# Three weight steps instead of one beside the samples' small mLSTM products, and a wait on two scored key groups ahead of decode's value loads

## The chip, the cores and the metric

The program runs on one core of a Trainium2 chip. The metric is device time in microseconds for one execution. TensorE (PE) multiplies matrices into PSUM banks, ScalarE (ACT) and VectorE (DVE) move and combine values, GpSimd (POOL) does elementwise work and issues some transfers, and SyncE (SP) issues most transfers. Each engine runs its own program in order; they meet at semaphores.

## The reference

One layer of a hybrid decoder on 512 prompt tokens and on 8 sequences of 8 new tokens each ("the samples", 64 rows). The parts that matter here, cut down:

```python
h = rmsnorm(x, g_pre_mix);  z = h @ w_in            # D_MODEL 1024; split into qa ka va qm km vm om, gates
# mLSTM branch, 4 heads of 128; for the samples one chunk of 8 tokens per sequence, with a state C0, n0, m0
A   = einsum('bthd,bshd->btsh', qc, kc) * wD
num = einsum('btsh,bshd->bthd', A, vc) + w_prev[..., None] * einsum('bhde,bthe->bthd', C, qc)
den = sum(A, axis=2) + w_prev * einsum('bhd,bthd->bth', n, qc)
hc  = num / maximum(abs(den), exp(-m_t))[..., None]
# attention of the samples: 2048 cached positions in 16 pages of 128 rows, found by a page table;
# blocks of 256 keys, the 3 best blocks by mean key are attended, plus the new tokens
s = einsum(q, cache_k[pages]) ; p = softmax(chosen blocks and own) ; out = p @ cache_v[pages]
# then both branches are merged by gates, and a squared-ReLU MLP follows
```

## The kernel before

All products with weights are done in three fp32r passes: a weight tile of 128x512 is loaded into one of four slots by SP, ACT rounds it to its high part (line 336), DVE subtracts to get the low part (line 347), and PE multiplies. This is one **weight step**. In the six chunks of `tokens_chunk` (keys, values, output gates of the mLSTM, then queries, keys, values of the attention: `TOKEN_CHUNKS`), a weight step is twelve 128x512 matmuls for the prompt (line 462) and two for the samples (line 470). There are 6 x 8 = 48 such steps. ACT and DVE prepare weights three steps ahead of PE.

The mLSTM itself is done beside these steps. It is written as three generators, one for each of PE, ACT and DVE (`pe_mlstm`, `act_mlstm`, `dve_mlstm`). After each weight step an engine runs its generator up to the next `yield`, so a `yield` is the place of one weight step, and what stands between two of them is one **piece**. The three generators must keep the same number of yields, so that what PE computes in a piece is read by ACT and DVE in theirs. The pieces use PSUM banks 5 to 7 in turn, in the order of a table (`M_USES`); the weight steps use banks 0 to 4. Two uses matter here: `sden` is the samples' denominators (lines 1400 and 1402), `snum` their numerators: four products of the weighted scores `sA` with the values `vm` (line 1407), then eight products with `sqC`, the state's share, four for each half "a" and "b" (line 1415). POOL runs its own list (`pool_mlstm`), released by semaphores.

Evictions of a whole chunk (`act_tokens`, `dve_tokens`) stand at every eighth step, whatever the pieces are. Late in the list ACT issues three output transfers for the samples' states (lines 1573 to 1576); while it issues them it rounds no weights.

After the projections comes the prompt's attention (`pe_prompt`), with matmuls of the gates woven in (line 897), and then decode, the samples' attention over the cache (`pe_decode`). Decode goes over 8 x 4 **groups** of four key pages, one group for each slot s. In slot s PE scores group s-1 (line 1935), transposes the four pages of group s (line 1926, in two halves), and six slots later multiplies with the values (line 1967). Keys lie in a ring `kring` of two groups, values in a ring `vring` of two groups. SP loads the keys of group s+2 when `k_free` says that group s is transposed:

```python
for s in range(DSLOTS):
    if s + 2 < ALL_GROUPS:
        eng.wait_ge(sem("k_free"), s + 1)
        pages(eng, cache_k, kring, "k_in", (s + 2) // GROUPS, (s + 2) % GROUPS)
    for r in fetched_in(A_SLOTS + s):
        sp_step(eng, n, r)
```

ACT copies a group's scores out of PSUM (line 2033) and raises `p_S` by one. POOL loads the values in `pool_values`, eight pages as soon as the prompt's attention is over (both halves of the ring are empty), and then four whenever PE frees a half (`v_free`). Nothing else stands behind these loads on POOL until the merge after decode. Each page is 128 rows of 2 KB, 256 KB in all, and its address is read from the page table at line 1891 before it is issued at line 1893.

Of the kernel before, what the change touches and what calls it, by code (L numbers as in the profile page):

```python
# [94 lines left out]
def moba_mlstm_step(  # L95
# [184 lines left out]
    def sem(name):  # L280
        if name not in names:
            names[name] = stack.enter_context(nc.semaphore(name))
        return names[name]
# [411 lines left out]
    def pe_project(eng, n):  # L695
        first_half_in(eng)
        features_chunk(eng, n, hT, KT, early={0: lambda: first_turn(eng, n, PT), EARLY - 1: lambda: second_half_in(eng)})
        features_chunk(eng, n, hT, KT, 1)
        for b in (5, 6, 7):
            eng.wait_ge(sem(f"free{b}"), n[f"free{b}"].value())  # L700
        side = pe_mlstm(eng)
        for _ in TOKEN_CHUNKS:
            tokens_chunk(eng, n, hT, KT, side=side)
        for _ in side:
            pass
        for b in (5, 6, 7):
            eng.wait_ge(sem(f"m_free{b}"), len(M_USES[b - 5::3]))
# [94 lines left out]
    def act_project(eng, n):  # L802
        for _ in range(KT):
            w_high(eng, n)
        for b in range(8):
            if b % 2 == 0:
                drain(eng, n, b)
                drained(eng.activation(qmT[:, b // 2, 0:HALFT], ps[:, b, 0:HALFT], ACT.Copy), n, b)
            else:
                skip(n, b, b == 7)  # L810
        for _ in range(KT):
            w_high(eng, n)
        eng.wait_ge(sem("small_in"), 64)
        for h in range(2):
            drain(eng, n, h, h == 1)
            c = slice(h * HALFT, (h + 1) * HALFT)
            eng.activation(rf[:, c], ps[32:32 + HM, h, 0:HALFT], ACT.Copy).then_inc(sem("r_in"), 1)
            drained(eng.activation(ri[:, c], ps[0:HM, h, 0:HALFT], ACT.Identity, bias=bif[:, 0:1]), n, h)  # L818
        side = act_mlstm(eng)
        for first in TOKEN_CHUNKS:  # L820
            for k in range(KT):
                w_high(eng, n)
                if k == KT - 1:
                    act_tokens(eng, n, first)
                next(side, None)
        for _ in side:
            pass
    def dve_project(eng, n):
        for _ in range(KT):
            w_low(eng, n)  # L830
        for b in range(8):
            if b % 2 == 1:
                drain(eng, n, b, b == 7)
                drained(eng.tensor_copy(qmT[:, b // 2, HALFT:NT], ps[:, b, 0:HALFT]), n, b)
            else:
                skip(n, b)
        for _ in range(KT):
            w_low(eng, n)
        for h in range(2):
            skip(n, h, h == 1)  # L840
        side = dve_mlstm(eng)
        for first in TOKEN_CHUNKS:
            for k in range(KT):
                w_low(eng, n)
                if k == KT - 1:
                    dve_tokens(eng, n, first)
                next(side, None)
        for _ in side:
            pass
# [363 lines left out]
    def m_bank(use):  # L1213
        return 5 + M_USES.index(use) % 3

    def m_take(eng, use):
        eng.wait_ge(sem(f"m_free{m_bank(use)}"), M_USES.index(use) // 3)
        return m_bank(use)

    def m_full(ins, use):  # L1220
        ins.then_inc(sem(f"m_full{m_bank(use)}"), 1)

    def m_read(eng, use):
        eng.wait_ge(sem(f"m_full{m_bank(use)}"), M_USES.index(use) // 3 + 1)
        return m_bank(use)

    def m_freed(ins, use):
        ins.then_inc(sem(f"m_free{m_bank(use)}"), 1)

    def m_emptied(eng, use):  # L1230
        eng.wait_ge(sem(f"m_free{m_bank(use)}"), M_USES.index(use) // 3 + 1)

    def heads_of(b, n, r=P):
        return ps[0:r, b, 0:HM * n].rearrange("p (h n) -> p h n", n=n)
# [7 lines left out]
    def pe_mlstm(eng):  # L1242
# [143 lines left out]
        for half in "ab":  # L1386
            b = m_take(eng, f"sqC{half}")
            for q in range(4):
                h, g = 2 * (half == "b") + q // 2, 4 * (q % 2)
                for j in range(4):  # L1390
# [11 lines left out]
        mm = eng.matmul(ps[:, b, 0:HM * NS], ones[:, :], sqn[:, :, :].rearrange("p h n -> p (h n)"),  # L1402
                        start=False, stop=True)
        m_full(mm, "sden")
        b = m_take(eng, "snum")
        for h in range(HM):
            eng.matmul(ps[:, b, h * NS:(h + 1) * NS], vm[0:NS, PT, h, 0:DM], sA[0:NS, h, :],
# [2 lines left out]
        for half in "ab":  # L1410
            m_emptied(eng, f"sqC{half}")
            for q in range(4):
                h = 2 * (half == "b") + q // 2
                c = h * NS + (q % 2) * 4 * S
                mm = eng.matmul(ps[:, b, c:c + 4 * S], sqC[:, int(half == "b"), q * P:(q + 1) * P], picked,
                                start=False, stop=(half == "b" and q == 3))
        m_full(mm, "snum")
        yield
        sample_update(0)
# [68 lines left out]
    def act_mlstm(eng):  # L1488
# [62 lines left out]
        yield  # L1551
        b = m_read(eng, "sden")
        m_freed(eng.activation(sden[:, :, :], heads_of(b, NS), ACT.Abs), "sden")
        yield
        yield
        numerator(0)
# [54 lines left out]
    def dve_mlstm(eng):  # L1611
# [160 lines left out]
        order(eng.tensor_tensor(sden[:, :, :], sden[:, :, :], se1[:, :, :], ALU.max))  # L1772
        order(eng.reciprocal(sden[:, :, :], sden[:, :, :]))
        yield
        b = m_read(eng, "snum")
        ins = eng.tensor_tensor(sden[:, :, :], heads_of(b, NS), sden[:, :, :], ALU.mult)
        m_freed(ins, "snum")
# [109 lines left out]
    def pages(eng, pool, ring, arrived, b, g):  # L1887

        flat = pool.rearrange("n p h d -> n p (h d)")
        for j in range(4):  # L1890
            page = eng.value_load(pt_sb[0:1, bass.ds(b * NPAGE + g * 4 + j, 1)],
                                  min_val=0, max_val=pool.shape[0] - 1)
            eng.dma_start(ring[:, 4 * (g % 2) + j, :], flat[bass.ds(page, 1), :, :].rearrange("a p n -> (a p) n"))\  # L1893
               .then_inc(sem(f"{arrived}{g % 2}"), 16)
# [13 lines left out]
    def pool_values(eng):  # L1908
        eng.wait_ge(sem("small_in"), 64)
        eng.wait_ge(sem("a_pv"), NSLOTS)  # L1910
        eng.tensor_copy(vown[:, :], tokA[0:NS, 2, PT, :]).then_inc(sem("v_own"), 1)
        eng.wait_ge(sem("v_own"), 1)
        eng.wait_ge(sem("kv_out"), 64)
        with eng.Fori(0, B) as b:
            for g in range(GROUPS):
                eng.wait_ge(sem("v_free"), b * GROUPS + g + 1)
                pages(eng, cache_v, vring, "v_in", b, g)
# [655 lines left out]
    with stack:  # L2573
# [13 lines left out]
        @block.gpsimd  # L2587
        def _(eng):
            constants(eng)
            eng.wait_ge(sem("normed"), TILES)  # L2590
            load_g(eng, g_post_mix)
            pool_mlstm(eng)
            pool_rotary(eng)
            pool_own_probs(eng)
            pool_values(eng)
            eng.wait_ge(sem("u_sum"), 16)
            load_x(eng, "x_back")
            eng.dma_start(g2B[:, :], g_pre_mlp.rearrange("(a n) -> a n", a=1).broadcast_to([P, D]))\
               .then_inc(sem("g2_in"), 16)
            eng.wait_ge(sem("normed"), 2 * TILES)  # L2600
            load_g(eng, g_post_mlp)
            eng.wait_ge(sem("turned_high"), 4 * TILES)
            eng.memset(wide[:, :, :], 0.0).then_inc(sem("y_zero"), 1)
# [81 lines left out]
```

## Time and profile before

| | |
|---|---|
| three runs | 1111.17, 1106.7, 1109.8 us; median 1109.8 |
| profiled execution, its own time | 1112.47 us |
| its span, first to last instruction | 1110.9 us |
| PE busy | 1070.9 us, 96% |
| DVE, ACT, POOL busy | 563.3, 449.3, 126.6 us |
| mean granted TensorE clock | 0.995 of full speed |
| read from memory, written | 141.62 MB, 7.10 MB |

The span lies 1.6 us inside the execution's own time. The profile counts an engine as busy while an instruction of it runs; a matmul's end is modelled. The granted clock is given as a share of 2.4 GHz: 1.00 is 2.4 GHz, 0.50 is 1.2 GHz. Times in rows are from the span's start.

### The profile page before, as it was taken

The page shows a single profiled execution, that of the slowest core. Times are in us where ns is not written, and L with a number is a line of the kernel's source. Part 1 is how long each engine was busy: PE and PEld are TensorE (multiplying, and loading weights), DVE is VectorE, ACT ScalarE, POOL GpSimd, SP SyncE. Part 2 cuts the span into 40 slices and gives each one's busy share as a digit, 9 for nine tenths or more (in the row PEclk, how much of TensorE's full clock was granted, in tenths as well). Part 3 has the DMA queues.
Part 4 walks back from the last instruction along what each step waited for, and adds up shares of the span by engine and source line. Part 5 has one row for each costly group of instructions (what it writes and reads, how often), then busy time and mean ns, then how long its engine had stood idle before and what let it go on. Part 6 is the DMA issues. An engine that isn't in the chain of part 4 may idle for free.

```text
span 1110.9 us, 20855 instructions
## 1 busy us (share of the span) xinstructions
PE 1070.9 (96%) x7672; PEld 913.8 (82%) x7672; DVE 563.3 (51%) x1227; ACT 449.3 (40%) x1023; POOL 126.6 (11%) x227
## 2 busy tenths in 40 slices
PE   7999999999999999999999998999999999999997
PEld 6977877887777777777789887998899899889985
DVE  5244534545675555665545748443344334443456
ACT  5353232324554455565542355441133214412441
POOL 4003110221001023333331100100000000000000
PEclk9999999999999999999999999999999999999999
DMA  7422216224135699999964441223222222222222
GB/s 218 119 83 58 67 48 134 67 76 133 41 86 181 199 322 332 329 338 337 323 203 134 151 134 39 86 84 96 78 86 77 86 82 80 85 81 81 77 86 85
DMA packets 93716, 150.02 MB, mean 135 GB/s; under 512 B 9377, under 2 KB 39590, under 8 KB 93622
## 3 DMA queue, kind: packets, MB, share of 16 engines
q1 hardware_dynamic: 75040, 103.83, 31.0%
q0 software_dynamic: 11968, 39.85, 10.7%
q10 hardware_dynamic: 6614, 5.06, 1.6%
q8 instruction: 61, 1.00, 0.4%
q14 instruction: 33, 0.27, 0.1%
HBM read 141.62 MB, written 7.10 MB: 134 GB/s over the span
## 4 chain that ended last, share of the span: by engine, by line
PE 78%; DVE 9%; DMA 4%; issue 3%; ACT 3%; SPq 1%; ACTq 1%; POOLq 0%; POOL 0%; DVEq 0%
PE ps L462 27%; PE ps L497 18%; PE ps L897 7%; PE ps L470 4%; PE ps L1926 4%; PE ps L913 3%; DMA kring<-in_cache_k_dram 3%; PE ps L435 2%; PE ps L1967 2%; PE ps L1935 2%; DVE xn L552 1%; PE ps L1061 1%; PE ps L1081 1%; DMA vring<-in_cache_v_dram 1%; PE ps L1951 1%
## 5 line engine op out<-in xcount | busy, mean ns | idle before, releaser
L347 DVE TENSOR_TENSOR w<-w,w 128x512 fp32r<-128x512 f32 (+1 forms) x240 | 167.9, 707 | 304.7 <-ACT w L336 300.3
L336 ACT ACTIVATE w<-w 128x512 fp32r<-128x512 f32 (+1 forms) x240 | 144.8, 613 | 336.8 <-PE ps L470 174.0
L497 PE MATMUL ps<-h2T,w 128*128 128x288 f32 x1536 | 208.3, 296 | 2.8 <-DVE wide L2540 1.7
L497 PEld LDWEIGHTS ps<-h2T,w 128*128 128x128 f32 x1536 | 205.4, 188 | 5.8 <-DVE wide L2540 2.4
L462 PE MATMUL ps<-w,hid 128*128 128x512 f32 x672 | 161.6, 389 | 0.0
L462 PE MATMUL ps<-w,hT 128*128 128x512 f32 x576 | 146.2, 403 | 1.4 <-ACT ri L818 1.4
L462 PEld LDWEIGHTS ps<-w,hid 128*128 128x128 f32 x672 | 125.9, 188 | 26.1
L462 PEld LDWEIGHTS ps<-w,hT 128*128 128x128 f32 x576 | 106.5, 191 | 26.7 <-issue 4.9
L897 PE MATMUL ps<-hT,w 128*128 128x288 f32 x768 | 126.8, 307 | 0.0
L897 PEld LDWEIGHTS ps<-hT,w 128*128 128x128 f32 x768 | 105.1, 188 | 12.3 <-issue 11.6
L1926 PEld LDWEIGHTS ps<-ident,kring 128*128 128x128 f32 x512 | 56.6, 141 | 39.3 <-DMA kring<-in_cache_k_dram 26.8
L1893 POOL DMA_DIRECT2D vring<-in_cache_v_dram x128 | 68.8, 538 | 174.6 <-issue 174.6
L2097 DVE COPY kT<-ps 128x512 f32<-128x512 f32 x64 | 44.1, 689 | 77.0 <-PE ps L1926 76.9
L1926 PE MATMUL ps<-ident,kring 128*128 128x128 f32 x512 | 68.4, 277 | 11.2 <-DMA kring<-in_cache_k_dram 7.4
L2027 ACT ACTIVATE kT<-ps 128x512 f32<-128x512 f32 x64 | 38.1, 595 | 32.4 <-PE ps L1926 32.3
L2043 ACT ACTIVATE sP<-sS,sbias 128x256 f32<-128x256 f32 x64 | 31.7, 498 | 24.7 <-DVE sbias L2129 24.7
L497 PE MATMUL ps<-hT,w 128*128 128x288 f32 x240 | 32.7, 296 | 3.2 <-DVE w L347 3.2
L1967 PE MATMUL ps<-vring,sPT 128*32 128x128 f32 x1024 | 34.6, 276 | 1.0 <-DMA vring<-in_cache_v_dram 1.0
L497 PEld LDWEIGHTS ps<-hT,w 128*128 128x128 f32 x240 | 32.0, 188 | 3.7 <-issue 1.9
L470 PE MATMUL ps<-w,hid 128*128 128x512 f32 x112 | 34.5, 389 | 0.0
L1935 PE MATMUL ps<-kT,qb 128*32 128x512 f32 x256 | 34.1, 605 | 0.0
L2461 ACT ACTIVATE hid<-rl 128x288 fp32r<-128x288 f32 x64 | 28.4, 444 | 8.1 <-DVE rl L2506 7.1
(356 smaller groups left out, 1291.1 us busy)
## 6 DMA issues: line engine op xcount, KB each, us to landing
kring<-in_cache_k_dram SPq DMA_DIRECT2D x128, 256.0 KB, 4.2
vring<-in_cache_v_dram POOLq DMA_DIRECT2D x128, 256.0 KB, 4.5
w<-in_w_in_dram SPq DMA_DIRECT2D x88, 256.0 KB, 2.9
w<-in_w_up_dram SPq DMA_DIRECT2D x64, 256.0 KB, 2.8
w<-in_w_down_dram SPq DMA_DIRECT2D x64, 256.0 KB, 2.9
w<-in_w_out_dram SPq DMA_DIRECT2D x16, 256.0 KB, 3.1
x<-in_x_prompt_dram SPq DMA_DIRECT2D x4, 512.0 KB, 7.2
out_dram<-sC ACTq DMA_DIRECT2D x1, 2048.0 KB
```

What stands on the lines that cost most here:

```text
L336: eng.activation(spread(w_hi, n, j, width), together(w32, n, j, width), ACT.Copy)\
L347: eng.tensor_tensor(spread(w_lo, n, j, width), together(w32, n, j, width), spread(w_hi, n, j, width).bitcast(F32), ALU.subtract).then_inc( ...
L462: mm = eng.matmul(ps[:, t, :], left[a][:, k, prompt_cols(t)], w[b][:, j, :], start=(k == 0 and (a, b) == THREE[0]), stop=(k == kt - 1 and ...
L470: mm = eng.matmul(ps[:, PT, :], left[2][:, k, T:NT + NS], w[b][:, j, :], start=(k == 0 and b == 0), stop=(k == kt - 1 and b == 1))
L497: mm = eng.matmul(ps[:, b, 0:HALFT], w[a][:, j, i * P:(i + 1) * P], right[c][:, k, h * HALFT:(h + 1) * HALFT], start=(k == 0 and (c, a) == ...
L897: mm = eng.matmul(ps[:, h, 0:HALFT], w[a][:, slots[part], (k % 4) * P:(k % 4 + 1) * P], hT[c][:, k, h * HALFT:(h + 1) * HALFT], start=(k = ...
L1893: eng.dma_start(ring[:, 4 * (g % 2) + j, :], flat[bass.ds(page, 1), :, :].rearrange("a p n -> (a p) n"))\
L1926: mm = eng.transpose(ps[:, 2 + h % 2, j * P:(j + 1) * P], kring[:, (m % 2) * 4 + j, h * P:(h + 1) * P], ident[:, :])
L1935: mm = eng.matmul(ps[32 * h:32 * h + 32, 4, :], qb[:, (m // GROUPS) % 2, h, :], kT[:, h, :], start=True, stop=True)
L1967: mm = eng.matmul(ps[32 * h:32 * h + 32, 6, 0:P], sPT[m % 2][:, j, 32 * h:32 * h + 32], vring[:, 4 * (m % 2) + j, h * P:(h + 1) * P], star ...
L2027: eng.activation(kT[:, h, :], ps[:, 2, :], ACT.Copy).then_inc(sem("p_kT_act"), 1)
L2097: eng.tensor_copy(kT[:, h, :], ps[:, 3, :]).then_inc(sem("p_kT_dve"), 1)
```

## The change

In each of the three generators two `yield`s are added at the samples' denominators and numerators, and POOL waits until ACT has copied out the scores of two key groups before it loads any values.

```diff
 # pe_mlstm
         m_full(mm, "sden")
+        yield
         b = m_take(eng, "snum")
         for h in range(HM):
             eng.matmul(ps[:, b, h * NS:(h + 1) * NS], vm[0:NS, PT, h, 0:DM], sA[0:NS, h, :],
...
         for half in "ab":
             m_emptied(eng, f"sqC{half}")
             for q in range(4):
...
                 mm = eng.matmul(ps[:, b, c:c + 4 * S], sqC[:, int(half == "b"), q * P:(q + 1) * P], picked,
                                 start=False, stop=(half == "b" and q == 3))
+            if half == "a":
+                yield
         m_full(mm, "snum")
         yield
         sample_update(0)
 # act_mlstm
         m_freed(eng.activation(sden[:, :, :], heads_of(b, NS), ACT.Abs), "sden")
+        yield
+        yield
         yield
         yield
         numerator(0)
 # dve_mlstm
         order(eng.reciprocal(sden[:, :, :], sden[:, :, :]))
         yield
+        yield
+        yield
         b = m_read(eng, "snum")
         ins = eng.tensor_tensor(sden[:, :, :], heads_of(b, NS), sden[:, :, :], ALU.mult)
 # pool_values
         eng.wait_ge(sem("kv_out"), 64)
+
+        eng.wait_ge(sem("p_S"), 2)
         with eng.Fori(0, B) as b:
```

On PE, the place of the samples' denominators (`ones` with `sA` and `sqn`) and numerators (`vm` with `sA`, `sqC` with `ident`), between weight steps (`w` with `hT`):

```order
 L1402 MATMUL ps<-sqn,ones 128x256
-L1407 MATMUL ps<-sA,vm 128x64 x4
-L1415 MATMUL ps<-ident,sqC 128x32 x8
+L462 MATMUL ps<-w,hT 128x512 x12
+L470 MATMUL ps<-w,hT 128x512 x2
+L1408 MATMUL ps<-sA,vm 128x64 x4
+L1416 MATMUL ps<-ident,sqC 128x32 x4
+L462 MATMUL ps<-w,hT 128x512 x12
+L470 MATMUL ps<-w,hT 128x512 x2
+L1416 MATMUL ps<-ident,sqC 128x32 x4
```

A weight step now stands between denominators and numerators, and another in the middle of the numerators; every later piece of the list stands two weight steps later.

On ACT, from the third piece's copy of numerators (`mnum`) to the eviction of the queries' chunk (`tokA`), before:

```order
94 L1508 ACTIVATE mnum_83<-ps 128x258 x2
95 L1573 DMA out_dram<-sC 128x32x128
96 L1575 DMA out_dram<-snn 8x512
97 L1576 DMA out_dram<-mlast 4x8x1
98 L336 ACTIVATE w<-w_117 128x512 x3
99 L1512 ACTIVATE mlT<-ps 128x4x128
100 L336 ACTIVATE w<-w_117 128x512
```

and now:

```order
95 L1511 ACTIVATE mnum_83<-ps 128x258 x2
96 L1578 DMA out_dram<-sC 128x32x128
97 L1580 DMA out_dram<-snn 8x512
98 L1581 DMA out_dram<-mlast 4x8x1
99 L336 ACTIVATE w<-w_117 128x512 x3
100 L750 ACTIVATE tokA<-ps 128x512 x2
101 L761 ACTIVATE tokA<-ps 64x512
```

The three output transfers and the three weight roundings behind them keep their order; the chunk's eviction, which does not move, now follows them directly.

On POOL, at the head of the loop that loads values, with the semaphores waited for, before:

```order
85 L1911 COPY vown<-tokA 64x512 [waits a_pv,small_in]
86 L1914 UNCONDITIONAL_BRANCH [waits kv_out,v_own]
87 L1914 ISA
88 L1891 ISA [waits v_free]
89 L1891 TENSOR_LOAD pt_sb
```

and now:

```order
85 L1918 COPY vown<-tokA 64x512 [waits a_pv,small_in]
86 L1923 UNCONDITIONAL_BRANCH [waits p_S,kv_out,v_own]
87 L1923 ISA
88 L1898 ISA [waits v_free]
89 L1898 TENSOR_LOAD pt_sb
```

Only the wait on `p_S` is new; nothing on POOL changes its place.

## Rows read from the trace of the kernel before

**Rows 1.** The page, part 1: busy time of each engine

```profile
PE 1070.9 (96%) x7672; PEld 913.8 (82%) x7672; DVE 563.3 (51%) x1227; ACT 449.3 (40%) x1023; POOL 126.6 (11%) x227
```

**Rows 2.** Who waited: PE, total us, times, longest us

```profile
PE ps L1926 <- DMA kring<-in_cache_k_dram: 7.4, 9, 1.6
...
PE ps L1297 <- DVE mnum L1631: 1.6, 1, 1.6
```

**Rows 3.** Busy time by stretch, then granted clock (PEclk), DMA share, GB/s

```profile
132.00:134.00 2.00, 2.00 (x16) 1.63 (x15) 1.14 (x2) 0.90 (x2) 0.00 (x0) 1.00 0.00 0
134.00:136.00 2.00, 2.00 (x13) 2.00 (x13) 1.94 (x3) 0.00 (x0) 0.00 (x0) 0.67 0.00 0
136.00:138.00 2.00, 2.00 (x6) 1.52 (x6) 0.22 (x1) 0.00 (x0) 0.00 (x0) 0.50 0.50 131
...
140.00:142.00 2.00, 2.00 (x7) 1.27 (x7) 0.00 (x0) 0.13 (x1) 0.00 (x0) 0.62 0.00 0
142.00:144.00 2.00, 2.00 (x9) 1.05 (x7) 1.07 (x2) 0.50 (x1) 0.00 (x0) 1.00 0.00 0
```

**Rows 4.** Timeline of PE at the samples' products: start, us, instructions

```profile
125.77 1.95 PE L1391 MATMUL ps<-sCT,sq 128*32 128x128 f32 x64
...
131.05 0.70 PE L1400 MATMUL ps<-sA,ones 64*128 64x256 f32 x2
...
132.30 1.10 PE L1407 MATMUL ps<-sA,vm 64*128 64x64 f32 x8
133.34 2.42 PE L1415 MATMUL ps<-ident,sqC 128*128 128x32 f32 x16
135.57 5.47 PE L462 MATMUL ps<-w,hT 128*128 128x512 f32 x12
...
141.71 1.13 PE L1312 MATMUL ps<-skw,vm 32*128 32x512 f32 x4
142.76 3.04 PE L462 MATMUL ps<-w,hT 128*128 128x512 f32 x12
...
146.09 1.05 PE L1277 MATMUL ps<-vm,mA 128*128 128x129 f32 x8
```

**Rows 5.** Timeline of PE: two weight steps with no piece between

```profile
247.56 2.88 PE L462 MATMUL ps<-w,hT 128*128 128x512 f32 x12
...
250.74 2.88 PE L462 MATMUL ps<-w,hT 128*128 128x512 f32 x12
```

**Rows 6.** Timeline of PE in decode: key groups 2 and 4, first values

```profile
359.39 1.07 PE L1935 MATMUL ps<-kT,qb 128*32 128x512 f32 x8
362.07 1.09 PE L1926 MATMUL ps<-ident,kring 128*128 128x128 f32 x8 [1.61 <-DMA kring<-in_cache_k_dram]
...
374.22 1.09 PE L1926 MATMUL ps<-ident,kring 128*128 128x128 f32 x8
...
391.14 1.08 PE L1967 MATMUL ps<-vring,sPT 128*32 128x128 f32 x32
```

**Rows 7.** The chain that ended last, the same place: start, us

```profile
352.54 0.36 SPq L1893
...
355.88 6.14 DMA kring<-in_cache_k_dram
```

**Rows 8.** Timeline of POOL: the first value pages' issues, first and last of eight

```profile
346.59 0.60 POOL L1911 COPY vown<-tokA 64x512 f32<-64x512 f32 x1 [81.31 <-PE ps L1081]
348.96 0.58 POOL L1893 DMA_DIRECT2D vring<-in_cache_v_dram  x1 [1.77 <-issue]
...
357.79 0.54 POOL L1893 DMA_DIRECT2D vring<-in_cache_v_dram  x1 [0.70 <-issue]
```

**Rows 9.** Timeline of ACT: the second group's scores copied

```profile
360.53 0.60 ACT L2033 ACTIVATE sS<-ps 128x512 f32<-128x512 f32 x1 [0.62 <-PE ps L1935]
```

**Rows 10.** Timeline of SP: groups 4 and 5, and weights ahead of them

```profile
362.31 0.98 SPq L312 DMA_DIRECT2D w<-in_w_in_dram  x2
366.37 9.72 SPq L1893 DMA_DIRECT2D kring<-in_cache_k_dram  x8
```

**Rows 11.** Issues of key pages at 366 to 372 us, median us to landing

```profile
kring<-in_cache_k_dram SPq DMA_DIRECT2D x4, 256.0 KB, 3.0
```

**Rows 12.** Key pages' time to landing, all issued from 300 to 500 us

```profile
DMA to landing us min/median/max: 2.6/4.1/7.1
```

## The prediction, made before the changed kernel was run

> **What bounds the kernel now.** I read the page first: PE is busy 1070.9 of 1110.9 us [rows 1]. So the time goes by what PE is given and how fast its clock runs; ACT, DVE and POOL matter where PE waits. Next I read who PE waited for. Two of its waits touch this change: keys in decode (9 waits, 7.4 us in all, the longest 1.6 us), and one wait of 1.6 us for DVE in the mLSTM's pieces [rows 2]. Then the granted clock by stretches of 2 us, since a busy PE can be a slow one. It is 1.00 up to 134, then 0.67, 0.50 and 0.62, and 1.00 again from 142 us on [rows 3]. The timeline shows what PE did before the fall: from 131.05 to 135.57 us it ran nothing but the samples' denominators and numerators, 28 short matmuls in 4.5 us, and the weight step behind them took 5.47 us for its first twelve matmuls where the next one took 3.04 [rows 4]. Last I read decode's start: PE ends the second group's scores at 360.46 (359.39 + 1.07) and idles 1.61 us for the keys of group 2 [rows 6]. The last page of that group was 6.14 us on its way [rows 7], beside eight value pages issued from 348.96 to 357.79 [rows 8].
>
> **Part one, the two weight steps.** No instruction is added or removed on PE, ACT or DVE. I price three things.
>
> The clock. At the low clock the weight step with its two sample matmuls lasted from 135.57 to 141.71, 6.14 us; the next one, at full clock and also followed by a piece, from 142.76 to 146.09, 3.33 us. That is 2.81 us. The end of the numerators was slow too: eight matmuls at line 1407 took 1.04 us (132.30 to 133.34), 0.13 each, so the sixteen at line 1415 should take 2.08 and took 2.23 [rows 4]. That is 0.15. If the clock stays up, 2.96 us come back. Why it should stay up: the longest stretch of short matmuls now is half the numerators, 1.04 + 1.04 = 2.1 us, where 4.5 us stood. The row nearest to it is line 1391, 1.95 us of short matmuls between two weight steps, after which the clock was still 1.00 at 132 us [rows 3, 4]. I take the whole 2.96; the low bound is nothing, if the clock falls anyway.
>
> More changes between weights and pieces. A weight step in front of a piece lasts 3.33 us to the piece's start, and 3.18 with none (250.74 - 247.56) [rows 4, 5]: 0.15 for each. Two more pieces stand alone now, so 0.30 is added. The bound below is 0.
>
> Everything later in the list is two steps later. Nothing runs dry at its end: the rows of two bare steps [rows 5] are of the five that followed the last piece; three stay. PE's 1.6 us wait for DVE [rows 2] comes from ACT's three output transfers, during which ACT rounds no weights; DVE waits for the weights and adds the state late. These transfers, the three roundings behind them and DVE's work keep their order among themselves, so I cost this at 0 and keep the wait. The queries' eviction stands behind them now, but it waits for PE's last step of the chunk anyway. Without that cover it would be the length of ACT's delay, once. The denominators' reciprocal on DVE gets more room, and no one waits for it before the samples' output, two steps later as well.
>
> Sum of part one: -2.96 + 0.30 = -2.66 us.
>
> **Part two, the wait ahead of the values.** The removed cost is the 1.61 us at group 2 [rows 6]. Its last page is issued at 355.88, 3.34 us after the group's first at 352.54 [rows 7]. With no values beside it such a page lands in about 3.0 us, as group 4's four pages did at 366 to 372 us [rows 11]: at 358.9, ahead of 360.46. So the wait goes whole.
>
> What is late next: the second group's scores are copied at 361.13 (360.53 + 0.60) [rows 9], since they lie before the wait. POOL then needs 1.77 us to its first issue, as it needed from 347.19 to 348.96, and issues eight pages every 1.26 us ((357.79 - 348.96) / 7) [rows 8]. The values are therefore issued from 362.9 to 371.7. They are not late for their own use, at 391.14 less 1.6 [rows 6]: even at the longest landing, 7.1 us [rows 12], the last is there at 378.8. On POOL only these eight issues are queued behind the new wait, and PE is the one that would wait for them.
>
> But now they meet group 4. SP began to issue it at 366.37 [rows 10]; 1.61 earlier is 364.76, its last page goes out 3.34 later, at 368.10, and PE wants it at 374.22 - 1.61 = 372.61 [rows 6]. Issued alone it lands at 371.1 and nothing is lost. At group 2's 6.14 us it lands at 374.24, and PE waits 1.63. At 7.1 us [rows 12] it waits 2.59. I take 6.14, since the picture is the same as at group 2: values flow from before the group's first page to after its last, here with the two weight tiles of 362.31 [rows 10] just ahead. So the wait moves by two groups: -1.61 + 1.63 = 0.0, with bounds -1.61 and +0.98.
>
> The Trainium skill says the same of the queues ("DMA: Bandwidth & Descriptors", "Issuing engines are not separate DMA queues"): transfers of whichever engine end up on the same 16 DMA engines and interleave. It speaks against a gain from the later issue on POOL unless the DMA engines are idle then; by it the sum of this part is 0, by row 11's landing alone it would be -1.61. The trace agrees with it: 6.14 us beside values, 3.0 without [rows 7, 11].
>
> **Sum.** -2.66 + 0.0 = -2.6 us. Against the profiled execution's own time, 1112.47, that gives 1109.8. The median of the runs lies 2.7 us below that execution, so on their scale the forecast is 1109.8 - 2.6 = 1107.2 us.
>
> **The rivals.**
>
> The key wait goes and none takes its place. For it: group 4's pages had over 1.5 us to spare (371.1 against 372.61). Against it: the values' eight pages lie right across it. Then -2.66 - 1.61 = -4.3 us: 1105.5.
>
> The low clock is an accident of the profiled execution. One trace shows one fall; the fall may come in some executions and not in others, whose median has then nothing to get back. For it: the three runs spread over 4.5 us, more than the 2.96 of one fall, and the profiled execution is slower than all three. Against it: a spread has other causes too. Time: the added 0.30 alone, 1110.1. The Trainium skill has a rule that leads here ("TensorE: Matmul & The Clock Gate", "Part 1: The HAM clock gate"): the monitor's window runs freely and does not start with the kernel, so the place of a clock change varies from run to run. One trace can't show that.
>
> The split does not keep the clock up. 2.1 us is a little longer than the 1.95 that left it at 1.00. The weight step after the denominators is whole, though, and that did not exist before. Time: again 1110.1.
>
> Slower: the values pile up on the weights, on group 3's end and on groups 4 and 5, as they are issued until 371.7. With 7.1 us to landing at group 4 and the same lag once more at group 5 the waits are 2 x 2.59 us, less 1.61: +3.6, with part one +0.9: 1110.7. It ends slower as soon as the new waits exceed 1.61 + 2.66 = 4.27 us. Against it: 7.1 us was the longest landing in all of that stretch [rows 12], and group 5 has SP's usual lead once POOL is done.
>
> **How the numbers follow.** Forecast (clock up, key wait moved) 0.42; key wait gone 0.15; fall not in the median's executions 0.27; clock falls anyway 0.08; pile-up 0.08. The likeliest gives 1107.2. The lowest sum is -2.96 - 1.61 = -4.6, 1105.2; the highest +0.30 + 0.98 = +1.3, 1111.1 without the clock's gain. The median of three runs that spread over 4.5 us can itself be off by a micro-second or more, so the range is 1104.0 to 1111.6. Half a per cent is 5.5 us, about what a measurement of this kernel can tell from no change. Faster than 1104.3 asks for the second case or a lucky median: 0.10. Slower than 1115.3 asks for more than the pile-up as priced: 0.03. The rest, 0.87, is within.
>
> **What would show it.** In the changed kernel's profile: granted clock 1.00 from 130 to 150 us; no weight step's twelve matmuls above 3.1 us there; steps to a piece still 3.3 us; the 1.6 us wait for DVE in place, some 3 to 4 us later (two bare steps less the gain). In decode: no wait at group 2; the first value page issued 1.8 us after the second scores' copy; group 4's last page near 6 us to landing, and a wait of about 1.6 us there. The prediction fails if the clock falls at another place, if the median is where it was, or if waits for keys sum to over 4 us more than now.

## The result, and the profile after

The changed kernel takes 1110.44 us (median of 12 runs, 1108.36 to 1113.13), the kernel before 1106.99 (12 runs beside it, 1105.64 to 1111.17). The ratio is 1.0027, 95% interval 1.0015 to 1.0039: slower by 3.0 us by the ratio, less than half a per cent, where I had forecast 2.6 us faster. The sign of the change is wrong. That the time still lies inside the forecast range is in part luck: the forecast was counted from 1109.8 us, the median of three runs of the kernel before, and twelve runs have 1106.99. Counted from that, the same range would have ended at 1108.8. The changed kernel's profiled execution took 1110.99 us, with a span of 1109.4 and a mean granted clock of 0.994.

The page, part 1, of the changed kernel, beside [rows 1]: nothing stands out.

```profile
PE 1071.9 (97%) x7672; PEld 915.2 (82%) x7672; DVE 563.3 (51%) x1227; ACT 449.0 (40%) x1023; POOL 126.4 (11%) x227
```

Who waited, PE's two rows that answer to [rows 2]. The waits for keys are fewer and the longest is longer; the wait for DVE in the mLSTM is kept.

```profile
PE ps L1935 <- DMA kring<-in_cache_k_dram: 4.2, 5, 2.4
...
PE ps L1297 <- DVE mnum L1636: 1.6, 1, 1.6
```

PE's timeline at the samples' products, beside [rows 4]: start, us, instructions. The denominators, the first half of the numerators and the second half (`sqC` "b") each stand between whole weight steps, and no step's twelve matmuls take longer than 3.10 us.

```profile
125.00 1.95 PE L1391 MATMUL ps<-sCT,sq 128*32 128x128 f32 x64
...
131.25 3.10 PE L462 MATMUL ps<-w,hT 128*128 128x512 f32 x12
...
135.76 1.08 PE L1416 MATMUL ps<-ident,sqC 128*128 128x32 f32 x8
136.68 3.01 PE L462 MATMUL ps<-w,hT 128*128 128x512 f32 x12
...
139.98 0.97 PE L1416 MATMUL ps<-ident,sqC 128*128 128x32 f32 x8
140.79 3.01 PE L462 MATMUL ps<-w,hT 128*128 128x512 f32 x12
...
148.55 1.05 PE L1277 MATMUL ps<-vm,mA 128*128 128x129 f32 x8
```

The windows of the same stretch (busy time of PE, PEld, DVE, ACT, POOL, then granted clock, DMA share, GB/s), beside [rows 3]: 1.00 where 0.67 and 0.50 stood.

```profile
134.00:136.00 2.00, 2.00 (x14) 1.54 (x13) 1.40 (x3) 0.63 (x1) 0.00 (x0) 1.00 0.02 3
136.00:138.00 2.00, 2.00 (x14) 1.78 (x14) 0.26 (x1) 0.00 (x0) 0.00 (x0) 1.00 0.75 163
```

So decode begins earlier, at 343.99 instead of 347.87. Of these 3.88 us, 0.77 were there ahead of the change (125.00 against 125.77 at line 1391); 3.11 came behind it. What becomes of the 3.88 us is in PE's timeline of decode, beside [rows 6]:

```profile
343.99 1.09 PE L1935 MATMUL ps<-ident,kring 128*128 128x128 f32 x8 [1.11 <-DVE attT L1183]
345.01 0.25 PE L1952 MATMUL ps<-kb,qb 128*32 128x8 f32 x8
345.19 3.08 PE L897 MATMUL ps<-hT,w 128*128 128x288 f32 x12
348.06 1.41 PE L1935 MATMUL ps<-ident,kring 128*128 128x128 f32 x8
...
358.06 1.09 PE L1935 MATMUL ps<-ident,kring 128*128 128x128 f32 x8
...
369.21 1.07 PE L1944 MATMUL ps<-kT,qb 128*32 128x512 f32 x8
372.67 1.96 PE L1935 MATMUL ps<-ident,kring 128*128 128x128 f32 x8 [2.40 <-DMA kring<-in_cache_k_dram]
374.56 0.30 PE L1952 MATMUL ps<-kb,qb 128*32 128x8 f32 x8
374.79 2.46 PE L897 MATMUL ps<-hT,w 128*128 128x288 f32 x12
...
391.10 1.08 PE L1976 MATMUL ps<-vring,sPT 128*32 128x128 f32 x32
```

The wait at group 2 (358.06) is gone. At group 4 a wait of 2.40 us stands in its place, and behind it the transposes take 1.96 instead of 1.09 and the gates' twelve matmuls 2.46 instead of about 1.85. The first values are multiplied at 391.10, where [rows 6] have 391.14: the whole lead is spent. The windows by microsecond (PE's busy time, clock, DMA share, GB/s) say why the work behind the wait is slow, and show a second place, at 345, that cost this one execution about 1.6 us:

```profile
345.00:346.00 1.00, 1.00 (x13) 0.71 0.06 16
346.00:347.00 1.00, 1.00 (x6) 0.50 0.00 0
...
372.00:373.00 1.00, 0.33 (x2) 0.86 1.05 375
373.00:374.00 1.00, 1.00 (x7) 0.50 0.99 361
374.00:375.00 1.00, 1.00 (x12) 0.50 0.98 337
```

The clock was at its lower level, 1.2 GHz, from about 373 to 376 us, at the end of the wait and behind it. Who was late is in the chain, beside [rows 7]: group 4's last page, issued at 366.09, took 6.54 us to land.

```profile
365.99 0.04 issue
366.09 6.54 DMA kring<-in_cache_k_dram
372.63 0.04 issue
372.67 1.96 PE ps L1935 x8
```

POOL's first and last value pages of the burst, beside [rows 8], lie across the whole of group 4's issue:

```profile
360.65 0.58 POOL L1900 DMA_DIRECT2D vring<-in_cache_v_dram  x1 [17.34 <-issue]
...
369.48 0.54 POOL L1900 DMA_DIRECT2D vring<-in_cache_v_dram  x1 [0.70 <-issue]
```

### The profile page after: what moved, and what is told of

It reads as the page before. It is cut to its first block, busy times and chain, and to the rows that moved or that the text cites. A ratio compares the mean times of both kernels' runs of the same rounds, so it can differ in the third digit from the quotient of the medians.

```text
span 1109.4 us, 20855 instructions
## 1 busy us (share of the span) xinstructions
PE 1071.9 (97%) x7672; PEld 915.2 (82%) x7672; DVE 563.3 (51%) x1227; ACT 449.0 (40%) x1023; POOL 126.4 (11%) x227
## 4 chain that ended last, share of the span: by engine, by line
PE 78%; DVE 8%; DMA 4%; issue 3%; ACT 3%; SPq 1%; ACTq 1%; POOLq 1%; POOL 0%; DVEq 0%
PE ps L462 27%; PE ps L497 18%; PE ps L897 7%; PE ps L1935 4%; PE ps L470 4%; PE ps L913 3%; DMA kring<-in_cache_k_dram 3%; PE ps L435 2%; PE ps L1944 2%; PE ps L1976 1%; PE ps L1061 1%; DVE xn L552 1%; PE ps L1081 1%; SPq L1898 1%; DVE w L347 1%
```

## The experiments

One measure serves for all of them beside the time: how long decode's start took in the profiled execution, from its first key transposes to its first product with values (in the changed kernel 391.10 - 343.99 = 47.11 us). What follows that product took 718.0 to 720.9 us in the thirteen profiles, and 718.3 in the changed kernel, so its loss does not lie there. A kernel's diff is against the changed kernel where nothing else is said. Ratios are to the kernel before, run on the same chip; differences in us between kernels of different chips go by these ratios.

### Each part alone

`e1_steps_only` is the changed kernel without the wait on `p_S`:

> The three weight steps beside the samples' products, without the wait ahead of the values. Theory A (the loss is the values' burst, moved onto key group 4): no wait above 1.7 us at group 2, none at group 4, clock 1.00 from 126 to 150 us, and a median 0.5 to 3 us below the kernel before, nearer to 1 if the low clock at 134 us is in only a part of the old kernel's executions. Rival B (the later pieces cost time that the sum left out): a median 2 to 4 us above the kernel before, with the loss seen ahead of 345 us. Rival C (where the clock falls is chance and both medians were drawn by it): within 1 us of the kernel before.

`e2_wait_only` is the kernel before with the one line

```diff
         eng.wait_ge(sem("kv_out"), 64)
+        eng.wait_ge(sem("p_S"), 2)
```

> The wait on two scored groups alone, the samples' products beside one step as before. Theory A: no wait at group 2, some 2.4 us at group 4 and a low clock of a few us behind it; a median 2 to 4.5 us above the kernel before. Rival B: within 1 us of the kernel before, since the loss lies in the pieces. Rival C: within 1 us.

The steps alone: 1107.77 us, ratio 0.9993 (0.9981 to 1.0006), so 0.8 us of gain that can't be told from none. The wait alone: 1111.8 us, ratio 1.0039 (1.0024 to 1.0054), so 4.3 us of loss. The two add up to +3.5, and +3.0 was measured: within the noise the parts simply add, and the loss is all of part two. The time of the steps alone fits theory A and rival C alike; the wait alone rules C out, and neither time fits B. PE's timeline of the wait alone, at groups 2 and 4, shows the changed kernel's picture again, a little worse:

```profile
358.19 1.09 PE L1928 MATMUL ps<-ident,kring 128*128 128x128 f32 x8
...
373.16 1.86 PE L1928 MATMUL ps<-ident,kring 128*128 128x128 f32 x8 [2.76 <-DMA kring<-in_cache_k_dram]
```

And the same of the steps alone: with the values in their old place, the wait at group 2 is 0.62 us and not 1.61.

```profile
358.27 1.09 PE L1933 MATMUL ps<-ident,kring 128*128 128x128 f32 x8 [0.62 <-DMA kring<-in_cache_k_dram]
```

### Is it the place of the burst?

```diff
-        eng.wait_ge(sem("p_S"), 2)
+        eng.wait_ge(sem("p_S"), 4)
```

and, as the second kernel, `p_S` 1 instead of 4.

> The changed kernel with the wait on four scored groups instead of two. Theory A: the burst of eight value pages starts some 12 us later, near 375 us, and meets the key group that is loaded then; groups 2 and 4 cost nothing, a wait of 1.5 to 2.5 us stands at group 6 instead, and the time is like the changed kernel's or up to 2 us less. If the lag was due to group 4 alone (the two weight tiles just ahead of it), there is no such wait and the time falls by 4 us against the changed kernel, below the kernel before.

> The changed kernel with the wait on one scored group instead of two, so the eight value pages start near 353 us, with group 2 already on its way and group 3 issued into the middle of them. By theory A (the group whose pages are issued behind a running burst pays) the wait of 2 to 3 us stands at group 3 instead of group 4, with a low clock behind it in some executions, and the median is within 1.5 us of the changed kernel. If it is the two weight tiles just ahead of the burst that make group 4 so late, group 3 waits under 1 us and the median is 2 us or more below the changed kernel.

Four groups: 1107.04 us, ratio 0.9992 (0.9977 to 1.0007). One of its twelve runs took 3651.64 us, which nothing here explains; the ratio leaves it out. One group: 1108.34 us, ratio 1.0002 (0.9991 to 1.0013). Neither shows the loss of two groups. With four, groups 2 and 4 don't wait, and a wait of 1.16 us stands at group 6. With one, two shorter waits take the place of the long one, and the clock stays up behind both:

```profile
363.29 1.09 PE L1935 MATMUL ps<-ident,kring 128*128 128x128 f32 x8 [0.63 <-DMA kring<-in_cache_k_dram]
...
371.15 1.09 PE L1935 MATMUL ps<-ident,kring 128*128 128x128 f32 x8 [1.74 <-DMA kring<-in_cache_k_dram]
```

The wait follows the burst wherever it is put, but both expectations had its price too high: 3.9 us below the changed kernel with four where 0 to 2 were expected, 2.8 below it with one where at most 1.5 were. The price goes by two times, that of a group's last page to landing and the lead, which is the time from that page's issue until PE has nothing else to do. At group 6 the page took 6.83 us, longer than the changed kernel's 6.54, and PE still waited only 1.16, since the lead there was 5.72 us and not 4.18.

The expectation for one group also named a rival, the two weight tiles that SP issues just ahead of group 4, and both of its marks came: under 1 us at group 3, and over 2 us below the changed kernel. The next experiment has these tiles in place too, and there group 4 does not wait, so they don't cause the wait by themselves. Whether they lengthen it beside the values was not tried.

### Is it the bytes, or the issues?

The first eight value pages carry 64 of their 512 columns, by the same eight issues at the same place. Left out are the other columns of the first two groups' values (the ring is set to zero ahead of the wait).

```diff
         eng.wait_ge(sem("p_S"), 2)
-        with eng.Fori(0, B) as b:
+        for g in range(2):
+            eng.wait_ge(sem("v_free"), g + 1)
+            pages(eng, cache_v, vring, "v_in", 0, g, 64)
...
-            eng.dma_start(ring[:, 4 * (g % 2) + j, :], ...
+            eng.dma_start(ring[:, 4 * (g % 2) + j, 0:w], ...
```

> The changed kernel whose first eight value pages carry 64 of their 512 columns (the rest of the ring is zeroed by POOL during its wait), so values of the first two groups are missing from the result; number, place and queue of the eight issues are unchanged, their bytes are an eighth. If group 4 is late through the bytes in flight, its wait (2.4 us) and the low clock behind it are gone, group 2 waits nothing either, and the median is 3 to 5 us below the changed kernel. If the issues themselves (descriptors, POOL's queue) hold SP's pages up, the wait stays above 1.5 us and the median within 1 us of the changed kernel.

1106.12 us, ratio 0.9991 (0.9978 to 1.0004). Group 4's transposes start at once, and the clock stays up. The DMA issues between 362 and 376 us (KB of each, median us to landing) of the changed kernel, and then of this one:

```profile
kring<-in_cache_k_dram SPq DMA_DIRECT2D x8, 256.0 KB, 4.9
vring<-in_cache_v_dram POOLq DMA_DIRECT2D x7, 256.0 KB, 4.9
```

```profile
kring<-in_cache_k_dram SPq DMA_DIRECT2D x10, 256.0 KB, 3.2
...
vring<-in_cache_v_dram POOLq DMA_DIRECT2D x5, 32.0 KB, 3.0
```

It is what the issues carry and not the issues: at an eighth of the size they leave the key pages at 3.2 us, near the 3.0 of [rows 11]. Bytes and packets are not told apart by this, since fewer packets came with the fewer bytes (POOL's queue moved 0.23 MB in 224 packets in this stretch, where the changed kernel's moved 2.10 in 640).

### Is it their density?

The eight pages keep their size but go out one at a time, each behind one of ACT's copies of transposed keys. There are two of these for each group, so the eight pages lie beside four groups and not beside two:

```diff
-        eng.wait_ge(sem("p_S"), 2)
-        with eng.Fori(0, B) as b:
+        for g in range(2):
+            eng.wait_ge(sem("v_free"), g + 1)
+            for j in range(4):
+                eng.wait_ge(sem("p_kT_act"), 2 + 4 * g + j)
+                pages(eng, cache_v, vring, "v_in", 0, g, (j,))
...
+        with eng.Fori(1, B) as b:
```

`e4_paced` is this in the changed kernel, `e5_paced_no_steps` in the kernel before, and `e11_paced_from_slot_2` has 4 instead of 2 in the line with `p_kT_act`.

> The changed kernel with the first eight value pages issued one for each key transpose that ACT copies out (one page every 3 us, from slot 1 on) instead of eight in 10 us behind one wait. Theory A: neither group 2 nor group 4 waits more than 0.5 us, the clock stays at 1.00 from 350 to 380 us, and the median is 3 to 6 us below the changed kernel, 0.5 to 3 us below the kernel before. Rival B: at or above the kernel before. If the burst's size doesn't matter but its presence beside any key group does, each group from 2 to 5 waits some 0.5 us and the time lies 1 us around the kernel before.

> The kernel before with nothing but the paced first value pages (one for each key transpose that ACT copies out). If the values' burst at decode's start costs the kernel before what its one wait at group 2 shows (0.6 to 1.6 us), this gains 0.5 to 1.5 us; the low clock near 134 us still comes in about half of the executions. If the kernel with steps and pacing gained by the steps alone, this stands within 0.5 us of the kernel before.

> The changed kernel with the paced first value pages, started one slot later (slot 2 to slot 5). If it is the pace that takes the waits away and not the place, no key wait above 0.7 us stands at groups 2 to 6, the clock stays up there, and the median is 0.5 to 2.5 us below the kernel before, as with pacing from slot 1. If pacing from slot 1 was lucky in its place, the median is within 0.5 us of the kernel before or above it.

Paced with the steps: 1106.67 us, ratio 0.9984 (0.9968 to 0.9999). Paced without them: 1106.23, ratio 0.9990 (0.9977 to 1.0003), which can't be told from none. Paced from one group later, with the steps: 1105.59 us, ratio 0.9979 (0.9969 to 0.9990). The last is 2.3 us faster than the kernel before by its ratio, the lowest of all versions; besides it only e4 and the later `e10_one_step_more` have intervals below 1, and the three intervals overlap. So pacing takes the changed kernel's loss away (4.8 us by the ratios of e4 and the changed kernel); that it gains anything over the old place of the values is not shown. In e11's profile group 4 does not wait. These are the 8 us from about the first issue of group 4 (PE's busy time, clock, DMA share, GB/s), with three value pages issued in them:

```profile
361.00:369.00 8.00, 8.00 (x65) 1.00 0.93 317
```

against the same 8 us of the changed kernel, with six:

```profile
362.00:370.00 8.00, 8.00 (x66) 1.00 1.03 360
```

### Is the slow clock a second cost of the wait?

PE is kept busy at group 4 with four products that nothing reads:

```diff
+            if s == 4:
+                for _ in range(4):
+                    eng.matmul(ps[:, 5, 0:CH], ident[:, :], kT[:, 0, :], start=True, stop=True)
```

> The changed kernel with four idle 512-column products (their result is never read) on PE just ahead of group 4's transposes, in the time in which it waits for the keys; some 2.1 us of PE work inside a wait of 2.4 to 2.8. They show what the clock's fall after the wait is worth: if it follows from the idle time, the clock stays at 1.00 from 372 to 378 us in this kernel, and the median is 0.5 to 1.5 us below the changed kernel's. If the fall is not bound to this wait, the median is that of the changed kernel or up to 0.5 us above it.

```profile
368.40 3.70 PE L2000 MATMUL ps<-kT,ident 128*128 128x512 f32 x8
371.94 1.04 PE L1935 MATMUL ps<-ident,kring 128*128 128x128 f32 x8
372.90 0.25 PE L1952 MATMUL ps<-kb,qb 128*32 128x8 f32 x8
373.08 1.87 PE L897 MATMUL ps<-hT,w 128*128 128x288 f32 x12
```

1110.65 us, ratio 1.0020 (1.0007 to 1.0033). The clock stayed up, and the work behind took its usual 1.04 and 1.87 us. But the filler lasted 3.5 us (371.94 - 368.40), 1.1 more than the wait it stood for, and that used up most of the 1.5 us that the clock gave back; by the ratios the time is 0.8 us below the changed kernel's, with intervals that overlap. So the profile shows, in one execution, the slow work behind the wait gone with PE's idleness, and the time does not confirm its price. The granted clocks of the runs bear the price out: their mean is 0.9971 here and 0.9958 in the changed kernel, 0.0013 x 1110 us = 1.4 us.

### How much are the steps worth?

`e9_longer_stretch` is the kernel before with the short stretch made longer (its `sample_update(0)` joined to the same piece), `e10_one_step_more` the kernel before with only one step added, between denominators and numerators.

```diff
 # e9, pe_mlstm
         m_full(mm, "snum")
-        yield
         sample_update(0)
+        yield
         yield
 # e10, pe_mlstm
         m_full(mm, "sden")
+        yield
         b = m_take(eng, "snum")
```

> The kernel before, with the first state update of the samples (four more short matmuls, 1.1 us) moved on PE alone into the same piece as denominators and numerators; a bare weight step follows in its old place. The stretch of short matmuls is then 5.6 us instead of 4.5. If the low clock at 134 us depends on how long that stretch is and on where the chip's look falls on it, it comes in more executions than in the kernel before: a mean clock of 0.994 to 0.995 over all runs against 0.996, and a median 0.5 to 2 us above the kernel before. If the clock has nothing to do with the stretch, clock and time are those of the kernel before.

> The kernel before with one weight step more instead of two: between the denominators and the numerators, which stay whole (a stretch of 3.3 us). If the fall depends on the stretch's length, it is rare here: mean clock 0.9965 or more as with two steps more, time 0.3 to 1.3 us below the kernel before. If only the full split keeps the clock up, the mean clock is 0.996 as before and the time too.

The longer stretch: 1107.22 us, ratio 0.9993 (0.9982 to 1.0003), no loss, and a mean clock of 0.9958 beside 0.9961 of the kernel before, so the 0.5 to 2 us of loss that were expected did not come. One step: 1106.54, ratio 0.9985 (0.9976 to 0.9994), 1.6 us of gain; the two steps' 0.8 lies within its interval. The profile of e10 shows the clock at 1.00 with 2.8 us of short products behind a whole weight step, and that of e9 shows it low behind 4.5 us, before the joined products even begin. They run slow inside the same fall (2.08 us, where they take 1.13 in [rows 4]):

```profile
132.48 2.33 PE L1415 MATMUL ps<-ident,sqC 128*128 128x32 f32 x16
134.74 2.08 PE L1312 MATMUL ps<-skw,vm 32*128 32x512 f32 x4
136.75 4.87 PE L462 MATMUL ps<-w,hT 128*128 128x512 f32 x12
```

In this profile the fall comes behind 4.5 us already, and the runs show nothing added by more of it.

### The thirteen profiles side by side

Worked out from PE's timeline of each: where decode starts, and how long its start takes. The last column gives the key waits in it.

| kernel | decode starts at, us | its start takes, us | key waits (group) |
|---|---|---|---|
| before | 347.87 | 43.27 | 1.61 (2) |
| e9, longer stretch | 346.87 | 41.80 | none |
| e1, steps only | 345.06 | 42.28 | 0.62 (2) |
| e10, one step | 343.79 | 41.71 | none |
| changed | 343.99 | 47.11, of which 1.6 from the clock at 345 | 2.40 (4) |
| e2, wait only | 345.65 | 45.92 | 2.76 (4) |
| e8, PE kept busy | 343.73 | 45.06 | filler |
| e6, wait for one | 343.97 | 44.10 | 0.63 (3), 1.74 (4) |
| e3, wait for four | 343.72 | 42.83 | 1.16 (6) |
| e7, small values | 343.53 | 42.03 | none |
| e4, paced | 343.34 | 42.09 | 0.44 (4) |
| e5, paced, no steps | 345.43 | 41.62 | none |
| e11, paced later | 343.88 | 41.62 | none |

The waits at single groups, from the chain and PE's timeline of each profile. Each wait is the time to landing less the lead, and some 0.04 us:

| kernel, group | last page issued at | to landing | lead | PE waits |
|---|---|---|---|---|
| before, 2 | 355.88 | 6.14 | 4.58 | 1.61 |
| e1, 2 | 353.08 | 5.15 | 4.57 | 0.62 |
| changed, 4 | 366.09 | 6.54 | 4.18 | 2.40 |
| e2, 4 | 366.22 | 6.90 | 4.18 | 2.76 |
| e6, 4 | 364.53 | 6.58 | 4.88 | 1.74 |
| e3, 6 | 376.42 | 6.83 | 5.72 | 1.16 |
| e4, 4 | 363.91 | 4.57 | 4.17 | 0.44 |

## Why the prediction was wrong, point by point

**The clock's 2.96 us: the mechanism held, its size was of one execution.** All four profiled executions without an added step (before, e2, e5, e9) have the clock fall between 132 and 142 us, and none of the nine with one or two added steps has it; from the state's products (line 1391, ahead of the change) to decode's start it is 218.9 to 219.0 us in all nine, 222.1 and 222.0 in before and e9, and 220.5 in e2 and e5. So the steps gained 3.1 us net in the profiled execution, and the fall was not always whole. The windows of e5 (PE's busy time, clock, DMA share, GB/s) add up to (1 - 0.86) x 4 + (1 - 0.71) x 4 = 1.7 us lost at full clock, e2's to as much, and [rows 3], with the same low clock in the two microseconds that they leave out, to 3.4; so do e9's.

```profile
132.00:136.00 4.00, 4.00 (x27) 0.86 0.03 3
136.00:140.00 4.00, 4.00 (x14) 0.71 0.23 62
```

The unprofiled runs bound it from the other side. The executions in whose profile no fall shows but the one in the last 10 us, which all thirteen have (e4, e6), have a mean clock of 0.998; 3.4 us lost of 1109 would leave 0.995. Of 95 runs of the kernel before, 45 have 0.997 or more and can't hold the whole fall (they can hold the half), and 31 have 0.995 or less. On their chip the steps alone had a mean clock of 0.9967 and the kernel before 0.9960: 0.0007 x 1108 us = 0.8 us, which is what the time shows. So the rival "an accident of the profiled execution", at 0.27, was half right, and by the times of e1 and e10 the term was worth some 0.8 to 1.6 us and not 2.96. By the Trainium skill ("TensorE: Matmul & The Clock Gate", "Part 1: The HAM clock gate") the monitor's window runs freely and does not start with the kernel; the runs agree as far as falls of the clock come in some executions and not in others in the same place, as the last section shows; a window they don't show.

**The switching of 0.30, the wait for DVE, the rest of part one: held.** Weight steps ahead of a piece last 3.30 to 3.48 us to the piece's start, and the wait for DVE is 1.6 us as before. The second step's 0.15 is too much, if anything: from line 1391 to decode e10 takes 218.92 us with one step and e1 218.99 with two.

**Group 2's wait, -1.61: right place, oversized.** It goes, as predicted. But it was 1.61, 0.62, 0 and 0 us in the four executions that have the values in their old place (before, e1, e10, e9), 0.56 on average. The profiled execution of before was again an unlucky one.

**Group 4's wait, +1.63: this is the step that failed.** The prediction took 6.14 us to landing "since the picture is the same as at group 2", and so had the wait move by two groups at a price of 0.0. Its mechanism was right: the wait did go to group 4, through values beside the keys. Its price was not, in two ways. First, the wait was 2.40 us and not 1.63, near my upper bound of 2.59; e2 had 2.76. About half of the difference is the landing, 6.54 instead of 6.14. The other half is the lead, 4.18 us instead of the 4.51 of the sum (372.61 - 368.10), because I took group 2's 3.34 us from a group's first issue to its last. Group 4 needed 3.73 (362.36 to 366.09), and in the kernel before it already needed 3.74 and not 3.34, which I could have read there:

```profile
370.11 0.34 SPq L1893 DMA_DIRECT2D kring<-in_cache_k_dram  x1
```

That PE came 2.34 us earlier than in the sum (370.27 for 372.61) cost nothing, since SP's issue came as much earlier (362.36 for 364.76). Second, what an idle of this length brings. The work behind it ran at the low clock and took about 0.87 + 0.6 = 1.5 us more (1.96 against 1.09, 2.46 against some 1.85). No term and no bound held that. So the part came to +2.6 (the mean of 2.40 and 2.76) + 1.5 - 0.56 = +3.5 us, where I had 0.0 and at most +0.98; the wait alone measured +4.3 (2.7 to 6.0). The filler was too long to confirm the 1.5 by time. The mean clocks of the runs say that the term is there, and not how large: against the same kernel without the wait the changed one has 0.9958 for 0.9967, 1.0 us, and the wait alone 0.9935 for 0.9960, 2.8 us.

**The pile-up.** I gave it 0.08 and priced it by waits at two groups. That the time came out near its 1110.7 is luck: the sum was another, one wait and the clock behind it.

**Bandwidth.** That transfers of two queues share what there is held: the collision moved along with the burst to groups 3 and 4 (wait for one), 4 (two) or 6 (four), went away with its bytes, and mostly went away when the burst was spread out.

## What to carry to other kernels

A burst of prefetches that is moved takes its collision along: ask which transfer it will lie across next and how much lead that one has, and try the burst spread out instead, one transfer for each step of the consumer: here that took the loss away, though it showed no clear gain by itself. A wait or a clock fall that is read from one execution is a sample, not the median: before it is counted as a gain, ask how often and how large it comes, from several runs' clocks or a second profile. And a wait of PE is not priced by its length alone, if it is long enough to bring the low clock behind it.

## What the runs showed of the hardware

A stall of the same length in the same place brings the low clock in some executions and not in others. Just after decode all thirteen profiles have PE idle for about 2.53 us ahead of the transposes of `xn`; in nine of them the clock falls there, in four (before, e4, e5, e6) it does not. Two of them, from PE's timeline, first e10 and then e4:

```profile
679.14 1.97 PE L2236 MATMUL ps<-ident,xn 128*128 128x128 f32 x8 [2.53 <-DVE xn L552]
```

```profile
678.80 1.09 PE L2248 MATMUL ps<-ident,xn 128*128 128x128 f32 x8 [2.54 <-DVE xn L552]
```

Idles of 2.40 and 2.76 us at group 4 brought it in both profiles that have them, and so did one of 1.90 us for keys at 485 us in e5; idles of up to 1.74 us did not. It also came with no idle at all, behind 4.5 us of short products (the row of e9 above), and once at 345 us, in the changed kernel, behind the idle of 1.11 us that all thirteen have there. The clock stayed low for about 3 to 7 us each time.

A key page of 256 KB took 3.0 us to land in the median with no values beside it, and 3.2 beside value pages of 32 KB. Beside a second queue of equal pages it took 4.9 in the median, and the last pages of the groups that waited took up to 6.9 (e2), while all 16 DMA engines were busy and moved about 360 GB/s.
